# Scores of two groups of heads as two row tiles of 64, in pairs, with one unpadded copy of the keys

## The reference

```python
scores = jnp.einsum("bnqkgd,bnskd->bnkgqs", q, kb).astype(jnp.float32) * scale
bias = -slopes[:, :, None, None] * jnp.abs(dist).astype(jnp.float32)
scores = jnp.where(valid[None, :, None, None], scores + bias[None, None], -jnp.inf)
m = jnp.maximum(jnp.max(scores, axis=-1, keepdims=True), sink_b)
p = jnp.exp(scores - m)
denom = jnp.sum(p, axis=-1, keepdims=True) + jnp.exp(sink_b - m)
o = jnp.einsum("bnkgqs,bnskd->bnqkgd", (p / denom).astype(v.dtype), vb)
```

## Time and profile before

| | |
|---|---|
| median of 3 runs | 1812.71 us (1812.69 to 1813.52) |
| span of the profiled execution, from first to last instruction | 1810.6 us |
| part of the median that lies outside that span | 2.1 us |
| PE busy | 1791.4 us, 99% |
| DVE busy | 885.3 us, 49% |
| ACT busy | 756.0 us, 42% |
| POOL busy | 1048.3 us, 58% |

### The profile page before, as it was taken

How to read it: one execution, slowest core, us unless ns; L and a number is a source line. 1 busy time by engine, 2 the same in 40 slices (tenths; PEclk the granted TensorE clock), 3 DMA queues, 4 the chain that set the end, 5 groups by cost and what they waited for, 6 DMA issues and landing times.

```text
span 1810.6 us, 23889 instructions
## 1 busy us (share of the span) xinstructions
PE 1791.4 (99%) x8208; PEld 1472.0 (81%) x8208; DVE 885.3 (49%) x1153; ACT 756.0 (42%) x1001; POOL 1048.3 (58%) x519
## 2 busy tenths in 40 slices
PE   9999999999999999999999999999999999999998
PEld 7888888888588888888888888888876888888887
DVE  7544442259966444432254444322898654444112
ACT  6333332246964333332243333222578643333222
POOL 5444457769566444457744444577775854444674
PEclk9999999999999999999999999999999999999999
DMA  4322223332113232233332232233211233222332
GB/s 174 111 98 93 94 78 96 107 109 66 48 59 105 94 102 93 83 82 100 118 103 97 93 99 86 81 97 118 85 53 48 88 102 101 93 95 82 87 96 70
DMA packets 53422, 166.70 MB, mean 92 GB/s; under 512 B 6000, under 2 KB 6256, under 8 KB 53360
## 3 DMA queue, kind: packets, MB, share of 16 engines
q1 hardware_dynamic: 52128, 163.78, 28.9%
q10 hardware_dynamic: 1232, 2.10, 0.3%
HBM read 163.76 MB, written 2.10 MB: 92 GB/s over the span
## 4 chain that ended last, share of the span: by engine, by line
issue 41%; POOL 31%; PE 24%; POOLq 2%; ACT 1%; DVE 1%; DMA 0%; ACTq 0%; DVEq 0%
POOL w_lo L431 26%; PE bank L1262 7%; PE bank L1263 7%; PE bank L1264 7%; POOL y_conv L482 2%; POOL sq_sum L440 2%; POOLq L430 1%; POOL x L540 1%; ACT prob L663 0%; PE bank L1448 0%; DVE bank L1030 0%; POOLq L444 0%; PE bank L1301 0%; PE bank L1436 0%; POOLq L451 0%
## 5 line engine op out<-in xcount | busy, mean ns | idle before, releaser
L431 POOL TENSOR_TENSOR w_lo<-stage,w_hi 128x1024 fp32r<-128x1024 f32 x352 | 866.3, 2462 | 697.7 <-ACT w_hi L559 697.6
L559 ACT ACTIVATE w_hi<-stage 128x1024 fp32r<-128x1024 f32 x352 | 372.5, 1060 | 882.0 <-PE bank L1264 880.7
L1262 PE MATMUL bank<-xs_hi,w_hi 128*128 128x512 f32 (+1 forms) x1696 | 657.5, 388 | 0.2 <-POOL w_lo L431 0.2
L1264 PE MATMUL bank<-xs_hi,w_lo 128*128 128x512 f32 (+1 forms) x1696 | 656.5, 387 | 0.0
L1263 PE MATMUL bank<-xs_lo,w_hi 128*128 128x512 f32 (+1 forms) x1696 | 656.4, 387 | 0.0
L1262 PEld LDWEIGHTS bank<-xs_hi,w_hi 128*128 128x128 f32 x1696 | 318.5, 188 | 66.6 <-issue 1.6
L1264 PEld LDWEIGHTS bank<-xs_hi,w_lo 128*128 128x128 f32 x1696 | 318.4, 188 | 64.8
L1263 PEld LDWEIGHTS bank<-xs_lo,w_hi 128*128 128x128 f32 x1696 | 318.5, 188 | 64.7
L885 DVE TENSOR_TENSOR work<-bank,rstd 128x512 f32<-128x512 f32 x176 | 120.5, 690 | 404.1 <-PE bank L1264 403.5
L1262 PE MATMUL bank<-h_hi,w_hi 128*128 128x512 f32 x704 | 273.9, 389 | 0.0
L1263 PE MATMUL bank<-h_lo,w_hi 128*128 128x512 f32 x704 | 273.9, 389 | 0.0
(11 more groups left out here) (166 smaller groups left out, 1202.6 us busy)
## 6 DMA issues: line engine op xcount, KB each, us to landing
stage<-w_gu SPq DMA_DIRECT2D x176, 512.0 KB, 3.3
stage<-w_down SPq DMA_DIRECT2D x64, 384.0 KB, 3.1
stage<-w_down SPq DMA_DIRECT2D x64, 320.0 KB, 2.9
stage<-w_in SPq DMA_DIRECT2D x24, 512.0 KB, 3.3
stage<-w_out SPq DMA_DIRECT2D x16, 512.0 KB, 3.3
x<-xT ACTq DMA_DIRECT2D x4, 512.0 KB, 6.6
stage<-w_in SPq DMA_DIRECT2D x8, 256.0 KB, 2.7
out<-result SPq DMA_DIRECT2D x8, 256.0 KB, 2.3
```

Source lines behind the costliest of these rows:

```text
L431: nc.gpsimd.tensor_tensor(w_lo[:, r, :], stage[:, r, :], w_hi[:, r, :].bitcast(F32), ALU.subtract).then_inc(split, 1)
L559: nc.scalar.activation(w_hi[:, r, :], stage[:, r, :], ACT.Copy).then_inc(hi_made, 1)
L1262: nc.tensor.matmul(to, wh, mh, start=first, stop=False)
L1264: return nc.tensor.matmul(to, wl, mh, start=False, stop=last)
```

## The change

- The keys are kept once: `k_hi` and `k_lo` are [128, 512], rows 0 to 63 the keys of group 0 and rows 64 to 127 those of group 1, as the `k` tile has them. The eight fills with zeros of the two layers go, and with them the semaphore `k_padded`; the copy on ACT and the subtraction on DVE are one instruction each, where they were two of 64 rows.
- The scores of the two groups for one c are computed together: six matmuls over 64 partitions each, alternately in row tile (0, 0) and row tile (64, 0) of PE's array, into two banks.
- The numbering of units changes to (b, c, kv), so that a pair is two successive units; PE now transposes two units, then computes two units' scores, then weighs or spreads what belongs to either.
- The probabilities' ring is addressed by the unit's number (`prob_slot`); DVE's and ACT's orders follow the new numbering.

```diff
-UNITS = [(g, c) for g in range(N_GROUPS) for c in range(GROUP)]
+UNITS = [(2 * b + kv, c) for b in range(NB) for c in range(GROUP) for kv in range(N_KV_HEADS)]
...
-            k_hi = sb("k_hi", [P, N_KV_HEADS, SEQ], F32R, region)
-            k_lo = sb("k_lo", [P, N_KV_HEADS, SEQ], F32R, region)
+            k_hi = sb("k_hi", [P, SEQ], F32R, region)
+            k_lo = sb("k_lo", [P, SEQ], F32R, region)
...
-                    for kv in range(N_KV_HEADS):
-                        rows = slice(HEAD_DIM * kv, HEAD_DIM * (kv + 1))
-                        nc.scalar.activation(k_hi[rows, kv, :], in_bank(t)[rows, :], ACT.Copy).then_inc(qk_hi, 1)
+                    nc.scalar.activation(k_hi[:], in_bank(t)[:], ACT.Copy).then_inc(qk_hi, 1)
...
-                for kv in range(N_KV_HEADS):
-                    other = slice(HEAD_DIM * (1 - kv), HEAD_DIM * (2 - kv))
-                    nc.vector.memset(k_hi[other, kv, :].bitcast(F32), 0.0).then_inc(k_padded, 1)
-                    nc.vector.memset(k_lo[other, kv, :].bitcast(F32), 0.0).then_inc(k_padded, 1)
...
-                def scores(g, c):
-
-                    b, kv = divmod(g, 2)
+                def scores(u):
+
+                    b, c = divmod(u // 2, GROUP)
                     first, n = keys_of(b)
-                    k = ATT["scores", g, c]
                     q, keys = slice(b * P, (b + 1) * P), slice(first * P, (first + n) * P)
-                    to = att_bank("scores", g, c)[:, 0:n * P]
                     tile_taken(IN_TILES.index(f"q{c}"))
-                    bank_taken(k)
-                    nc.tensor.matmul(to, q_hi[:, c, q], k_hi[:, kv, keys], start=True, stop=False)
-                    nc.tensor.matmul(to, q_hi[:, c, q], k_lo[:, kv, keys], start=False, stop=False)
-                    nc.tensor.matmul(to, q_lo[:, c, q], k_hi[:, kv, keys], start=False,
-                                     stop=True).then_inc(scored, 1)
+                    to = []
+                    for g in (2 * b, 2 * b + 1):
+                        bank_taken(ATT["scores", g, c])
+                        to.append(att_bank("scores", g, c)[:, 0:n * P])
+                    for i, (of_q, of_k) in enumerate([(q_hi, k_hi), (q_hi, k_lo), (q_lo, k_hi)]):
+                        for kv in range(N_KV_HEADS):
+                            rows = slice(HEAD_DIM * kv, HEAD_DIM * (kv + 1))
+                            made = nc.tensor.matmul(to[kv], of_q[rows, c, q], of_k[rows, keys], start=i == 0, stop=i == 2,
+                                                    tile_position=(HEAD_DIM * kv, 0))
+                            if i == 2:
+                                made.then_inc(scored, 1)
...
-                for u, (g, c) in enumerate(UNITS):
-                    turn_weights(g, c)
-                    if u + LEAD < N_UNITS:
-                        scores(*UNITS[u + LEAD])
-                    if u == 0:
+                for pair in range(0, N_UNITS, 2):
+                    turn_weights(*UNITS[pair])
+                    turn_weights(*UNITS[pair + 1])
+                    if pair + LEAD < N_UNITS:
+                        scores(pair + LEAD)
+                    if pair == 0:
                         pe.wait_ge(v_made, l + 1)
-                    if u in WEIGH_AT:
-                        weigh_values(*WEIGH_AT[u])
-                    if u in SPREAD_AT:
-                        spread_denominators(SPREAD_AT.index(u))
-                    if u == 28:
-                        channel_mean()
+                    for u in (pair, pair + 1):
+                        if u in WEIGH_AT:
+                            weigh_values(*WEIGH_AT[u])
+                        if u in SPREAD_AT:
+                            spread_denominators(SPREAD_AT.index(u))
+                        if u == 28:
+                            channel_mean()
```

More of the change, by code:

```diff
@@ L99 @@
 N_UNITS = N_GROUPS * GROUP
-UNITS = [(g, c) for g in range(N_GROUPS) for c in range(GROUP)]
+UNITS = [(2 * b + kv, c) for b in range(NB) for c in range(GROUP) for kv in range(N_KV_HEADS)]
+UNIT_NO = {unit: u for u, unit in enumerate(UNITS)}
 LEAD = 3 * GROUP
@@ L113, in attention_turns @@
     turns = [("scores", *unit) for unit in UNITS[:LEAD]]
-    for u, unit in enumerate(UNITS):
-        turns.append(("turned", *unit))
+    for u in range(0, N_UNITS, 2):
+        turns += [("turned", *unit) for unit in UNITS[u:u + 2]]
         if u + LEAD < N_UNITS:
-            turns.append(("scores", *UNITS[u + LEAD]))
-        if u in SPREAD_AT:
-            turns.append(("spread", SPREAD_AT.index(u), 0))
+            turns += [("scores", *unit) for unit in UNITS[u + LEAD:u + LEAD + 2]]
+        if u + 1 in SPREAD_AT:
+            turns.append(("spread", SPREAD_AT.index(u + 1), 0))
     return {turn: n for n, turn in enumerate(turns)}
@@ L758, in _ @@
                         high_attention(u - 25, 0)
-                    if c == 0 and g >= 4:
-                        mix_high(12 + g - 4)
+                    if u % GROUP == 0 and u >= N_UNITS // 2:
+                        mix_high(12 + (u - N_UNITS // 2) // GROUP)
                 square_channels(3)
@@ L1052, in bias_scores @@
                     nc.vector.tensor_tensor_reduce(
-                        out=probs[g % PROBS][:, c, 0:n * P], in0=att_bank("scores", g, c)[:, 0:n * P],
+                        out=prob_slot(g, c)[:, 0:n * P], in0=att_bank("scores", g, c)[:, 0:n * P],
                         in1=dist[:, at:at + n * P], scale=slope(kv, c),
@@ L1100, in _ @@
                     done += V_SPREAD[t]
-                for c in range(3):
-                    bias_scores(0, c)
+                for unit in UNITS[:3]:
+                    bias_scores(*unit)
                 taps(done, V_SPREAD[13])
                 done += V_SPREAD[13]
-                bias_scores(0, 3)
-                bias_scores(1, 0)
-                bias_scores(1, 1)
+                for unit in UNITS[3:6]:
+                    bias_scores(*unit)
                 in_summed(13)
                 nc.vector.tensor_tensor(work[:, V_SLOT, :], in_bank(13)[:], rstd[:], ALU.mult).then_inc(evicted, 3)
[L1110 to L1114, removed]
+                for unit in UNITS[6:LEAD]:
+                    bias_scores(*unit)
                 taps(done, 2)
@@ L1432, in turn_weights @@
                     k = ATT["turned", g, c]
[L1433 removed]
+                    pe.wait_ge(exped, l * N_UNITS + UNIT_NO[g, c] + 1)
                     bank_taken(k)
@@ L1533, in _ @@
                 half_tile(12, 1)
-                pe.wait_ge(k_padded, l * 5 + 5)
-                for c in range(3):
-                    scores(0, c)
+                scores(0)
                 half_tile(13, 0)
-                scores(0, 3)
-                scores(1, 0)
-                scores(1, 1)
+                scores(2)
+                scores(4)
                 half_tile(13, 1)
-                scores(1, 2)
-                scores(1, 3)
-                scores(2, 0)
+                scores(6)
+                scores(8)
                 tile_taken(13)
```

55 lines of the change are left out of this document (26 added, 29 removed).

## The result

The changed kernel takes 1819.41 us (median of 12 runs, 1815.38 to 1821.34) against 1812.74 of before (12 runs, 1812.48 to 1813.58). The ratio is 1.0032, with an interval of 1.0024 to 1.0040: slower by 6.7 us, outside the range of the prediction. The spread is news by itself: 6 us instead of 1.1. The profiled execution is the longest of the twelve, 1821.34 us with a span of 1819.5.

What follows compares the result with a forecast made beforehand. ACT was taken to bound the attention, DVE close behind. Per layer +0.6 by the last units, -0.4 in the tail, +0.1 for the later `v` tile: +0.3, twice, on 1812.7, so 1813.3 us; 8-in-10 range 1810.0 to 1818.5.

Steps and rivals of the forecast that it cites:

- PE's scores matter only where one of the two stands waiting for them: Attention, 448.6 to 490 us: ACT sets the pace, DVE close behind; DVE's waits for scores are 0.32 and 0.22 us.
- What the new order adds: Attention: pairs wait for both banks and PE runs less far ahead of DVE; +0.3 us a layer in sum.
- The clock: Closing sign, attention stage: the prediction is wrong if the granted clock falls there; no size or chance given.
- A pair on PE: Scores of two units: six weight loads one after another, 0.66 us for both widths; bounds 0.54/0.36 and 1.08/0.72.
- PE's own time stays nearly the same: Attention, per layer: 3.8 us saved on pairs, 3.0 added by mode changes; bounds -4.2 and +3.0.
- Changes of mode: PE between whole array and tiles: each change drains the pipeline for 0.15 us, 20 more a layer, 3.0 us.
- The lump: PE work between pairs 22, 23 and 24, 25: DVE's tap starts 0.8 us later, about 0.6 reaches ACT.
- The tail: End of attention, 485.94 to 491.23: fewer mode changes and two calls in one piece save 0.4 us a layer.
- No cover: Rival, attention: PE's saving reaches the end, 4.2 us a layer, 1804.3 us in all; chance 0.07.
- tiles that don't overlap: Rival, score pairs: 1.4 us to `scored`, +2.2 us a layer, 1817.1 us in all; chance 0.2.
- a drain at each alternation: Rival, score pairs: pipeline empties between row tiles, 2.7 us a pair, +12 us a layer, 1837 us; chance 0.05.
- The coupling costs more: Rival, attention loop: each of ten pairs loses 0.2 to 0.3 us, +2.5 a layer, 1817.7 us; chance 0.08.

Runs made afterwards that it cites:

- e7: Kernel before, order and whole array kept, with the third score matmul (low part of the queries) left out: 1810.93 us, ratio 0.9990.
- e8: Kernel before, order and whole array kept, with two of the three score matmuls left out: 1810.90 us, ratio 0.9991.
- e10: As e1 (whole array, padded keys, new numbering), but PE alternates one unit's transposes and one unit's scores as before: 1812.63 us, ratio 0.9999.
- e1: Changed kernel, but each score matmul over the whole array on zero-padded keys, as before: 1821.89 us, ratio 1.0047.
- e2: Changed kernel plus four unused matmuls of zeros over the whole array ahead of each pair from unit 12 on: 1830.90 us, ratio 1.0098.
- e3: Changed kernel with some weigh_values calls moved later, so that no two stand together before the tail: 1815.60 us, ratio 1.0016.
- e12: As e1, with the low part of the queries left out, so that a pair is four matmuls: 1817.60 us, ratio 1.0024.
- e4: Order of before, unit by unit, with keys kept once and each unit's three score matmuls in its own row tile: 1816.83 us, ratio 1.0023.
- e9: Kernel before, except that from unit 24 on PE transposes two units, then weighs values for both: 1812.26 us, ratio 0.9998.
- e11: Changed kernel with a pair's matmuls issued three in the first row tile, then three in the second: 1818.89 us, ratio 1.0033.

## Why the prediction was wrong

**The step that failed is the one from ACT's busy share to "PE's scores matter only where one of the two stands waiting for them".** That is true of the order of before, as e7 and e8 show, and of e10. I carried it over to the new order, where it isn't: e1 against e10 puts 9.3 us on PE's order by twos, and in e2 more than half of what is added to PE ahead of a pair comes out at the end. Two terms of the sum were wrong by it:
- "What the new order adds" had +0.6 us by the last units and +0.3 for a layer. Measured at full clock it is 1.12 us at unit 29. For the end of the stage I estimate 1.2 to 1.5: from unit 29 on, layer one of e3 adds 0.1 and layer one of e1 0.4, both without a fall.
- The clock had nothing. In the profiled execution the falls then have 1.3 to 1.6 us of layer one's 2.8 and 4.3 to 4.6 of layer two's 5.8.

The order's part, 2.4 to 3.0 us for two layers, would have given 1815.1 to 1815.7 us, inside the range. The falls took the time out of it. They are 3.7 to 4.3 of the median's 6.7 us, by the same estimate; e12's one run at 0.999, 1815.14 us, agrees with 2.4 for the order.

**The cause.** PE's two waits ahead of a pair, for DVE and for ACT, end close together, and PE stands behind both in the loop: for units 14 and 15 the bias of unit 12 ends at 459.33, `keep_turned(1)` at 459.63, and the pair starts at 459.73; in eight of the nine pairs of layer one the two ends are 0.05 to 0.62 us apart. PE now waits longer there and its work is shorter, so it is busy for less, and its clock falls. With little running ahead, a fall can reach the end. Its price is not one number. In 3.4 us at half clock PE does 1.7 us less, and of this 1.5 us come out in e3 and 1.6 in e1, both late in the stage. But the first fall of layer two of the changed kernel, at 11 us into the stage, had cost 0.6 us by unit 17 (1360.85 - 1344.18 = 16.67 us, for 465.02 - 448.96 = 16.06 in layer one). The changed kernel's runs go the same way, 1815.4 to 1817.4 us at clocks of 0.997 to 0.998 and 1818.7 to 1821.3 at 0.994 to 0.995. PE's order by twos is shown as the cause by e1 and e10, the part of the lumps by e3, the price of a fall by the two layers of e1 and of e3, and that tiles aren't needed for any of it by e12. That the clock falls because PE is busy for less is what e2 (more work, no fall) and e8 (less work, falls in the old order) speak for.

Point by point:
- **A pair on PE.** Predicted 0.66 us for both widths, by loads one after another; measured steps of 0.18 and 0.12 us, that is 0.54 and 0.36, the lower bound. The loads of both tiles run side by side. The Trainium skill's rule for a pack ("TensorE: Matmul & The Clock Gate", Part 3), one matmul's time plus 4 ns a tile, was right where I preferred to add up loads: the trace agrees, with 0.18 us for two matmuls where one alone takes 0.18 too. So "PE's own time stays nearly the same" was wrong as well, and it hid the risk for the clock: PE's busy time went from 29.89 to 23.93 of 32 us.
- **Changes of mode.** Predicted 0.15; measured 0.18 in and 0.09 out in e4. Right.
- **The lump.** DVE's wait at unit 24 is 0.61 us, for 0.8 to 1.1 predicted, at 26 0.66 for some tenths. The tap ahead of unit 24 starts 472.99 - 448.96 = 24.03 us after the first exponential, for 23.19 before: 0.84 later, for 0.8 predicted. In part this is luck, as the pair 22, 23 started 0.3 us later than worked out and the rest took 0.3 less. What it does to the clock was missing. I placed it at units 10 and 11, and with the clock down the second, at 18 and 19, was the dear one: there 1.91 us of ACT's time go.
- **The tail.** 494.40 - 489.33 = 5.07 us against 5.29: 0.22, for 0.4 predicted; e9 has 0.2 too.
- **Rivals.** "No cover" is refuted by e7 and e8, "tiles that don't overlap" and "a drain at each alternation" by the rows of step 0.18. "The coupling costs more" came nearest, with its place right. Its time of 1817.7 came near by luck: it had 2.5 us a layer for the coupling alone, where 1.2 to 1.5 were measured and estimated with the lump inside, and the falls made up the rest. I gave it 0.08.
- **The clock** stood in the last sentence as what would make the prediction wrong, and it did. It had no price and no chance. The bounds of a pair already allowed PE 4.2 us less work a layer while ACT kept the pace, so a sinking share of busy time was in reach. That it would bring the clock down no row of before could show.

Open: a layer of the changed kernel without a fall was not caught, why falls differ from run to run and from layer to layer isn't explained, no smaller filler than e2's was tried, and the order of before with all its products was never seen with a fall.

## What to carry to other kernels

Engines that are busy for 98% of a stage don't make the others free: ask how many steps the others run ahead, and what is left of that after the change. Here a batch of two on one engine in a loop of three took away one step of lead. And giving TensorE less to do inside a stage that others bound can lower its clock; whether that costs anything depends on the slack that it has there.

## What the runs showed of the hardware

- Two row tiles of 64x128 in fp32r run side by side, loads and matmuls, at 0.18 us for two of 384 columns, and in e11 without neighbouring in the program.
- Entering a row tile from the whole array and leaving it again cost 0.18 and 0.09 us in e4.
- A mean clock of 0.997 over 1815 us hides stretches at half clock; a page in 40 slices shows 9 in each. Stretches of 2 to 4 us show it.
- In e8's profile the clock was at half for 6.8 us in each layer, and the stage was 47.1 us, for 47.2 in e7's, whose attention had no fall. Late in a tight stage 3.4 us cost 1.5 to 1.6 us (e3, e1), earlier in the changed kernel 0.6.
